# A hybrid decoder step on one core: where the first three gate tiles of the up-projection stage are computed

## The reference

```python
h = rmsnorm(x, g_mix)
proj = h @ w_in
qkv, gdn_gate, b_raw, a_raw, z, xbc, dt_raw, gate_a, gate_b = split_cols(proj, IN_SPLITS)
...
o_a, gdn_S_new = gated_delta_chunked(q, k, v, g, beta, gdn_S)     # 8 heads, chunks of tokens
o_a = rmsnorm(o_a, gdn_norm_w) * silu(gdn_gate)
...
merged = sigmoid(gate_a) * (o_a @ w_gdn_up) + sigmoid(gate_b) * (y_b @ w_ssm_up)
x = x + merged @ w_out
```

## Time and profile before

| | |
|---|---|
| median of 3 runs | 3571.55 us (3570.78 to 3578.92) |
| the profiled execution | 3571.93 us, span 3570.2 us |
| PE busy | 3376.4 us, 95% of the span |
| DVE, ACT, POOL busy | 1687.7, 1024.4, 972.3 us |
| mean granted clock | 0.956 |

### The profile page before, as it was taken

The page is one execution under the profiler, slowest core; times in us unless marked ns, Lnnn a source line. Parts: engine busy times, 40 slices in busy tenths (PEclk is TensorE's granted clock), DMA queues, the critical chain, the costliest instruction groups (busy, mean ns, idle before and its releaser), DMA issues.

```text
span 3570.2 us, 54760 instructions
## 1 busy us (share of the span) xinstructions
PE 3376.4 (95%) x21375; PEld 3230.8 (90%) x21375; DVE 1687.7 (47%) x2656; ACT 1024.4 (29%) x2240; POOL 972.3 (27%) x438
## 2 busy tenths in 40 slices
PE   8899999998899999999999988999889999999998
PEld 7889998988799999999998977999758999999998
DVE  5655566565310057877787853132243242323133
ACT  5333233333221133344444333021231110101010
POOL 3221222221112221221122101213323444444442
PEclk9999999998899999999999999999888999999999
DMA  4111011111032222333332256223121111111111
GB/s 131 50 43 43 22 44 42 48 42 36 19 119 72 78 82 57 89 86 85 86 84 76 80 162 213 71 95 101 49 110 42 48 48 47 46 43 47 47 47 66
DMA packets 339221, 249.59 MB, mean 70 GB/s; under 512 B 13652, under 2 KB 320413, under 8 KB 339029
## 3 DMA queue, kind: packets, MB, share of 16 engines
q1 hardware_dynamic: 323310, 228.32, 21.4%
q10 hardware_dynamic: 15792, 19.60, 1.5%
HBM read 201.57 MB, written 46.78 MB: 70 GB/s over the span
## 4 chain that ended last, share of the span: by engine, by line
PE 74%; DVE 14%; ACT 4%; issue 4%; DMA 3%; POOL 1%; ACTq 0%; DVEq 0%; SPq 0%; POOLq 0%
PE psum L1467 8%; PE psum L1469 8%; PE psum L1468 8%; PE psum L1026 8%; PE psum L1028 8%; PE psum L1027 8%; PE psum L1152 4%; PE psum L1321 2%; PE psum L1323 2%; PE psum L1322 2%; DVE arena L2194 2%; PE psum L1143 1%; PE psum L1529 1%; PE psum L1281 1%; DMA slab<-in_w_in_dram 1%
## 5 line engine op out<-in xcount | busy, mean ns | idle before, releaser
L1026 PE MATMUL psum<-xh,whe 128*128 128x344 f32 x2304 | 785.9, 341 | 8.7 <-POOL wle L2999 5.1
L1027 PE MATMUL psum<-xl,whe 128*128 128x344 f32 x2304 | 752.3, 327 | 0.0
L1028 PE MATMUL psum<-xh,wle 128*128 128x344 f32 x2304 | 751.8, 326 | 0.0
L2999 POOL TENSOR_TENSOR wle<-slab,whe 128x1024 fp32r<-128x1024 f32 x104 | 262.9, 2528 | 1467.5 <-ACT whe L1618 1467.5
L1026 PEld LDWEIGHTS psum<-xh,whe 128*128 128x128 f32 x2304 | 448.8, 195 | 13.5 <-issue 6.2
L1027 PEld LDWEIGHTS psum<-xl,whe 128*128 128x128 f32 x2304 | 448.9, 195 | 0.6
L1028 PEld LDWEIGHTS psum<-xh,wle 128*128 128x128 f32 x2304 | 446.8, 194 | 0.0
L3089 POOL TENSOR_SCALAR wparts<-slab 128x1024 fp32r<-128x1024 f32 x80 | 221.9, 2773 | 500.9 <-POOLq L68 500.9
L1467 PE MATMUL psum<-at,wparts 128*128 128x344 f32 x960 | 307.9, 321 | 5.2 <-DVE r L2908 5.2
L1469 PE MATMUL psum<-at,wparts 128*128 128x344 f32 x960 | 306.7, 319 | 0.0
L1468 PE MATMUL psum<-xlow,wparts 128*128 128x344 f32 x960 | 306.2, 319 | 0.0
(11 more groups left out here) (420 smaller groups left out, 6604.7 us busy)
## 6 DMA issues: line engine op xcount, KB each, us to landing
slab<-in_w_in_dram SPq DMA_DIRECT2D x96, 512.0 KB, 3.9
arena<-d_rows SPq DMA_DIRECT2D x40, 512.0 KB, 5.5
slab<-in_w_ff_up_dram SPq DMA_DIRECT2D x32, 512.0 KB, 3.9
slab<-in_w_ff_down_dram SPq DMA_DIRECT2D x32, 512.0 KB, 3.6
out_dram<-arena SPq DMA_DIRECT2D x24, 512.0 KB, 4.5
arena<-in_state_ssm_dram SPq DMA_DIRECT2D x16, 512.0 KB, 6.0
d_yb<-arena SPq DMA_DIRECT2D x16, 512.0 KB, 4.6
slab<-in_w_ssm_up_dram SPq DMA_DIRECT2D x16, 512.0 KB, 3.7
```

What stands on the lines that cost most here:

```text
L1026: pe.matmul(out, w_hi, a_hi, start=(k == 0), stop=False)
L1027: pe.matmul(out, w_hi, a_lo, start=False, stop=False)
L1028: mm = pe.matmul(out, w_lo, a_hi, start=False, stop=(k == KT - 1))
L2999: pool.tensor_tensor(rounded(wle[slot]), slab[slot][:, :], whe[slot], ALU.subtract).then_inc(wlo_ready, 1)
```

## The change

Three tables of work move. (1) The last head gets its own table `LAST_FILL`: 24 steps in its front (8, 6, 6, 4), none in levels and decode, 3 in each scan chunk. Its first tile (u = 0) is thus computed in the front, u = 1 in the scan chunks; a chunk's three steps are split, one ahead of the state update and two at its end. ACT empties these tiles inside the head (`gate_tile`), and issues the first `d_gateb` store there. (2) PE announces the end of the head, computes the third tile (u = 2) and only then waits for the barrier; up_a begins with u = 3. (3) SP asks for slabs 2 and 3 ahead of the barrier, ACT and POOL prepare slab 2 in the third level, and the eight stored outputs are asked for in a row behind it, the eighth behind a wait of its own; only ACT waits for their landing. `tgate` and `gbst` take a place that is free in the last head.

```diff
         sd_ready = sem("sd_ready")
-        oa_ready, oa_stored, oa_loaded, oah_ready, oal_ready = (
-            sem(n) for n in ("oa_ready", "oa_stored", "oa_loaded", "oah_ready", "oal_ready"))
+        oa_ready, oa_stored, oah_ready, oal_ready = (
+            sem(n) for n in ("oa_ready", "oa_stored", "oah_ready", "oal_ready"))
+        oa_loaded = [sem(f"oa_loaded{i}") for i in range(2)]
...
         oraw = carve(KT * NT).rearrange("p (k t) -> p k t", k=KT)
-        tgate = [carve(NT) for _ in range(2)]
+        assert cut[0] <= raw_at
+        cut[0] = raw_at
+        tgate, gbst = zip(*[(carve(NT), carve(NT)) for _ in range(2)])
         mgst = [carve(NT) for _ in range(2)]
-        gbst = [carve(NT) for _ in range(2)]
...
-        def fills(step):
-
-            n = lambda s: FILL[s.rstrip("0123456789")]
+        LAST_FILL = {"rw": 8, "norm": 6, "turn": 6, "kkqk": 4, "scan": 3, "decode": 0, "level": 0}
+
+        def fills(step, table=FILL):
+
+            n = lambda s: table[s.rstrip("0123456789")]
             i = STEPS.index(step)
             return sum(n(s) for s in STEPS[:i]), sum(n(s) for s in STEPS[:i + 1])
...
             sp.wait_ge(sdec_stored, (GH_N - 1) * 16)
             sd_load(GH_N - 1)
+            upa_slab(0, 2)
+            upa_slab(0, 3)
             sp.drain().then_inc(phase_done, 1)
             sp.wait_ge(phase_done, 10)
-            sp.wait_ge(oa_stored, 16 * GH_N)
-            for part_ in range(2):
-                for k in range(4 * part_, 4 * part_ + 4):
-                    sp.dma_start(oraw[:, k, :], d_oa[k]).then_inc(oa_loaded, 16)
-                    if k % 4 == 3:
-                        sp.wait_ge(oa_loaded, 16 * (k + 1))
-                upa_slab(0, 2 + part_)
+            sp.wait_ge(oa_stored, 16 * (GH_N - 1))
+            for k in range(KT):
+                if k == KT - 1:
+                    sp.wait_ge(oa_stored, 16 * GH_N)
+                sp.dma_start(oraw[:, k, :], d_oa[k]).then_inc(oa_loaded[k // 4], 16)
             upa_slab(0, 4)
...
+
+            def gate_steps(m0, m1):
+
+                project_parts(0, W_UPA, m0, m1, lambda u, n: (
+                    proj_taken, A_UPA + n - 2 if u == 0 else A_UPA + 3 * (u - 1) + n + 1), 4 * [(xh, xl)])
+
             def body(h, more):
                 def fill(step, part=None):
+                    a, z = fills(step, FILL if more else LAST_FILL)
+                    if part is not None:
+                        mid = (a + z) // 2
+                        a, z = ((a, mid), (mid, z))[part]
                     if more:
-                        a, z = fills(step)
-                        if part is not None:
-                            mid = (a + z) // 2
-                            a, z = ((a, mid), (mid, z))[part]
                         qkvg(h + 1, a, z)
+                    else:
+                        gate_steps(a, z)
...
@@ -1191,8 +1203,6 @@
                     if c % 4 == 3:
                         mm.then_inc(bank_full[7], 1)
                     fill(f"scan{c}", 1)
-                    if not more:
-                        project_parts(0, W_UPA, 3 * c, 3 * c + 3, lambda u, n: (proj_taken, A_UPA), [(xh, xl)])
...
             body(GH_N - 1, False)
+            pe.drain().then_inc(phase_done, 1)
+            gate_steps(48, 72)
             pe.wait_ge(oa_ready, GH_N)
-            pe.drain().then_inc(phase_done, 1)
             pe.wait_ge(phase_done, 10)
...
-                project_parts(6 * pair, W_UPA, 24 if first else 0, 6 * 24, before, 4 * [(xh, xl)] + 2 * [(oah, oal)],
+                project_parts(6 * pair, W_UPA, 72 if first else 0, 6 * 24, before, 4 * [(xh, xl)] + 2 * [(oah, oal)],
...
+            def gate_tile(pair, u, n):
+
+                tg = (gbst if u % 2 else tgate)[u // 2]
+                act.wait_ge(proj_full, 18 * pair + (3 * (W_UPA + u) + n + 1))
+                act.activation(tg[:, n * GW:(n + 1) * GW], psum[:, n, 0:GW], ACT.Tanh, scale=0.5).then_inc(proj_taken, 1)
+                if u % 2 and n == 2:
+                    act.wait_ge(proj_taken, 12 * pair + (A_UPA + 3 * u + 3))
+                    act.dma_start(d_gateb[bass.ds(2 * pair + u // 2, 1)].rearrange("o p t -> p (o t)"), gbst[u // 2]
+                                  ).then_inc(gateb_stored[u // 2], 16)
+
             def body(h, first, more):
                 def evac(step):
+                    a, z = fills(step, FILL if more else LAST_FILL)
                     if more:
-                        a, z = fills(step)
                         evacuate(h + 1, a // 8, z // 8)
+                    else:
+                        for m in range(a // 8, z // 8):
+                            gate_tile(0, m // 3, m % 3)
...
-                    if more and S == 3:
-                        high_weights((4 * h, 7))
+                    if S == 3:
+                        high_weights((4 * h, 7 if more else 6))
...
-                for u in range(6):
+                def outputs_high(part_):
+                    act.wait_ge(oa_stored, 16 * GH_N)
+                    act.wait_ge(oa_loaded[part_], 16 * 4)
+                    for k in range(4 * part_, 4 * part_ + 4):
+                        act.activation(rounded(oah[:, k, :]), oraw[:, k, :], ACT.Copy).then_inc(oah_ready, 1)
+
+                for u in range(2 if first else 0, 6):
                     for n in range(3):
...
-                            act.wait_ge(proj_full, 18 * pair + (3 * (W_UPA + u) + n + 1))
-                            ins = act.activation(tg[:, n * GW:(n + 1) * GW], psum[:, n, 0:GW], ACT.Tanh, scale=0.5)
-                            ins.then_inc(proj_taken, 1)
-                        if n == 0 and not (first and u == 0):
+                            gate_tile(pair, u, n)
+                        if n == 0:
                             high_weights((6 * pair, W_UPA + u + 1))
-                    if u < 4 and u % 2:
-                        act.wait_ge(proj_taken, 12 * pair + (A_UPA + 3 * u + 3))
-                        act.dma_start(d_gateb[bass.ds(2 * pair + u // 2, 1)].rearrange("o p t -> p (o t)"), gbst[u // 2]
-                                      ).then_inc(gateb_stored[u // 2], 16)
-                    if first and u < 2:
-                        for k in range(4 * u, 4 * u + 4):
-                            act.wait_ge(oa_loaded, 16 * (4 * u + 4))
-                            act.activation(rounded(oah[:, k, :]), oraw[:, k, :], ACT.Copy).then_inc(oah_ready, 1)
+                        if first and (u, n) in ((2, 2), (3, 0)):
+                            outputs_high(u - 2)
...
                     if more and S in (2, 3):
                         low_weights((4 * h, 4 + S))
+                    elif S == 3:
+                        low_weights((4 * h, 6))
...
-            for u in range(2, 6):
+            for u in range(3, 6):
```

More of the change, by code:

```diff
@@ L1821, in gates @@
             def gates(pair, first, last):
-                for u in range(6):
+                def outputs_high(part_):
[4 more added lines that the diff above has]
+                for u in range(2 if first else 0, 6):
                     for n in range(3):
                         if u < 4:
-                            tg = (gbst if u % 2 else tgate)[u // 2]
                             if n == 0 and not first:
```

## The result

| | before | changed |
|---|---|---|
| median, 6 runs each | 3580.27 us (3570.78 to 3587.14) | 3554.61 us (3548.27 to 3560.91) |
| profiled execution | 3571.93 us, span 3570.2 | 3548.69 us, span 3547.0 |
| ratio | | 0.9936, 95% interval 0.9922 to 0.9950 |

The kernel is faster by 0.64%, some 23 us (the two medians differ by 25.7). I had said 3543.0 us, 3539 to 3551, and 28.7 us. The direction was right; the time lies outside the range. (Lines of the changed kernel: rw L1119, levels L1155, new values L1184, state update L1196, transposes of the output L1231, projection steps L1030 to L1032, the tanh L1748, ACT's rounding of slabs L1629 and of outputs L1852, POOL's `wle` L3020.)

The account below looks back on a forecast made before the run. PE was taken to bound the stage behind the first output tiles (busy 225.70 of 225.70 us), so its lateness there stays. -2.94 - 4.1 + 0.55 - 22.2 = -28.7 us against 3571.93 gave 3543; range 3539 to 3551.

Parts of the forecast that it names:

- Part 1: Last head's front: 24 steps (11.3 us of PE) hidden at no cost, clock stays up, first level 9.00 us: -2.94 us.
- The rule that speaks against it: Front and first level: short bursts between waits each start at the lower clock, so the first level keeps 11.94 us.
- Part 2: Last head's scan chunks: one step fills the wait ahead of the state update, a chunk takes 2.60 us: -4.1 us.
- Part 3: Third level: ACT's rounding of slab 2 ahead of its copies of w gives PE w later: +0.55 us.
- Part 4: End of head: u = 2 ahead of the barrier, u = 3 at once, u = 4 starts at 998.1, not 1020.30: -22.2 us.
- 1: Front, first level: clock still falls, 2.94 us later, 3545.8; with a longer slow piece in u = 2 up to 3548; alone 0.22.
- 2: Before u = 4: late landing or ACT's order replaces the stall, 2 to 5 us wait, 3545 to 3548; chance 0.14.
- 3: Last head's front: the steps are not hidden, all 11.3 us come onto DVE's and POOL's chain, 3554; chance 0.06.
- 4: up_a: another bound than PE makes up the difference, nothing comes of the change, 3571.5; chance 0.04.
- 5: up_a, tiles u = 2 to 5 and next pair: a stretch at 1.2 GHz follows, making the kernel slower; chance 0.02.
- Sum: Whole kernel: four parts give -28.7 us against the profiled 3571.93, so 3543.2; median 0.4 below that execution, so 3542.9.
- The range: Whole kernel: 3539 (favourable bounds, less 1.5 us for clock pieces elsewhere) to 3551 (both first rivals).

Follow-up runs that it names:

- scan_unsplit: The changed kernel with a scan chunk's three steps all behind the state update, none ahead of it; ratio to before 0.9939.
- outputs_in_turn: The changed kernel with the stored outputs asked for four and four behind the last store, each four waited for, then slab 4; ratio to before 0.9958.
- tail_prep16: The changed kernel with 16 steps of u = 2 moved into the last head's tail and slab 3 prepared inside the head; ratio to before 0.9942.
- outputs_early: The kernel before, with SP asking for the first seven stored outputs without waiting for the last store to land; ratio to before 0.9986.

## Why the prediction was right or wrong

- **Part 1, first level (-2.94).** 11.94 to 9.21 in the first profiles: -2.73. Over all profiles before has 11.4 on average (10.4 to 11.9), so about -2.2. "I cost them at nothing" held for the steps; in two of three profiles of the changed kernel the front was 1.3 to 1.6 us longer behind a late slab, which no term allowed for.
- **The rule that speaks against it.** In seven of ten profiles twenty-four steps between waits kept the whole front at 1.00, in three the clock fell for 3 to 3.5 us within the second group, behind the longer wait for ACT; the levels had 1.00 in all. By the rule of the Trainium skill (TensorE: Matmul & The Clock Gate, section HAM oscillation — how this bites in real kernels) each burst would have started at the lower clock again; in the first profile none in the front did.
- **Part 2, scan chunks (-4.1).** -3.78: a chunk is 2.69 us, not 2.60, as the part behind the state update is 1.72 and not 1.62. scan_unsplit gives 3.55 us of it to the split.
- **Part 3 (+0.55).** Third level and w took 11.39 against 10.86: +0.53.
- **Part 4 (-22.2).** -23.0 in the first profiles: the restart cost 0.27 us, and the slow piece of u = 2 was 2.4 us (970.36 to 972.76) instead of 3.7. `wle` came 2.7 us ahead of its use, and DVE's last remainder at 996.0, some 1.5 us ahead. Over all profiles part 4 gives 47.5 - 25.9 = 21.6.
- **The rivals.** 1: in the first profile the clock did not fall in the front; in the other two it did for a part of it, and the first level took 9.2 us all the same. 2: no landing took the stall's place in the changed kernel; it did in outputs_in_turn and tail_prep16. 3: the front grew by 1.6 us at most, of 11.3, and that behind a late slab. 4 and 5: up_a kept the clock (1.00 in 994.20 to 1223.00).
- **The step that failed** is the one under "Sum": "-28.7 us against the profiled execution's 3571.93", and "The median of the runs is 0.4 below that execution". The first profiles do differ by 28.85 in the stretch, but that one of before was the longest of six. A term of the sum was the draw of one execution: 5.06 us of stall behind a store of 4.97, where the stall was 2.44 us in another profile. The mean of six stretches of before less the mean of three of the changed kernel is 146.3 - 119.8 = 26.4 us. By its parts: first level -2.2, front +1.25, scan chunks -3.8, part 3 +0.5, tail -0.6, behind the transposes -21.6. That the first profiles came within 0.2 us of the sum was in part luck.
- **The reference point** failed more heavily. All runs of the kernel before, 78 of them, have a mean of 3578.5 us (standard deviation 4.3, 3567.8 to 3587.1); the three shown with the prediction (mean 3573.8) and the profiled one stood on the low side. Twelve runs of the changed kernel have a mean of 3553.4 (4.2). The difference is 25.1 us, with 1.3 of standard error, which agrees with 26.4 and no longer with 28.7. Why those first four ran low is open. Of the 11.6 us by which 3543.0 missed the median, some 7 are this reference, 2.3 the long draw, and the rest scatter.
- **The range** allowed 1.5 us "for clock pieces elsewhere that fall differently". It should have had the scatter of the runs on both sides: 4.3 us for one and, for the median of three, an estimated 2.9 (two thirds of it). The mechanism of all four parts held; what failed is the level and the size.

## What to carry to other kernels

Take the level of the forecast from all runs and the saving from rows, and before a stall is entered as a term, ask which part of it is fixed and which is a landing that varies. Work for the busiest engine that goes into its own waits cost nothing here, and it kept the clock up in the stage behind. When steps are moved ahead of a barrier, put the stores that release the barrier ahead of the copies that empty the new tiles: here that was worth 1 us.

## What the runs showed of the hardware that I had not expected

**Identical code, other times.** Ahead of the stretch nothing differs, yet it starts anywhere from 871.80 to 887.9 us. The windows of two profiles of the kernel before:

```profile
0.00:871.80 871.80, 810.57 (x5596) 767.82 (x5597) 519.60 (x930) 334.36 (x847) 203.62 (x122) 0.95 0.16 49
```

```profile
0.00:885.90 885.90, 823.13 (x5597) 776.22 (x5597) 520.66 (x930) 334.53 (x847) 203.38 (x122) 0.93 0.16 48
```

Same instructions, 0.95 and 0.93 of the clock, 14.1 us. Over 68 of the 78 runs of the kernel before the time follows the granted clock of the whole run: 3584.4 us at 0.951 (8 runs), 3581.4 at 0.952 (13), 3579.0 at 0.953 (18), 3576.8 at 0.954 (15), 3574.1 at 0.955 (8), 3571.8 at 0.956 (6). What decides how long the pieces at 1.2 GHz are in one run is open; I did not try it.

**A store's landing.** The store of 516 KB took 2.67, 2.67, 4.41, 4.62, 4.97 and 5.06 us in six profiles of one kernel. In all seventeen profiles its length goes with the one packet of 16 KB on the "instruction" queue. Where none lies beside the store it takes 2.7 to 3.0 us (nine profiles, the three of the changed kernel with 3.0 among them, though the loads of the others already run beside it there). With one of 1.0 us it takes 3.5 or 3.6 (the three with more steps in the tail), and with one of 1.3 to 1.9 us it takes 4.4 to 5.1 (four of before and outputs_early). What sets when that packet comes I did not try. In the changed kernel only the eighth load waits for the store, and with it ACT's rounding.
